# A mixture-of-experts layer whose tokens are selected by products on TensorE instead of gathered

## The reference

```
h2 = RMSNorm(x) * (1 + scale2) + shift2
lg = h2 @ w_rg                       # 4 groups: top 1
le = h2 @ w_re[group]                # 8 experts in the group: top 2
gates = softmax(lg)[group] * softmax(top 2 of le)
for each expert e with its tokens:
    hdn = silu(xe @ w_gate[e]) * (xe @ w_up[e])     # 1024 -> 512
    y   = hdn @ w_down[e]                            # 512 -> 1024
x += gate2 * sum of gates * y over each token's two experts
```

## Time and profile before

| | |
|---|---|
| time, median of 2 runs | 1788.38 us (1786.84 to 1789.93) |
| the profiled execution | 1790.88 us, span 1789.1 us, mean granted clock 0.967 |
| TensorE products, weight loads | 1587.5 us (89%), 769.3 us (43%) |
| VectorE, ScalarE, GpSimd | 716.6 us (40%), 434.7 us (24%), 160.1 us (9%) |
| HBM read, written | 520.96 MB, 23.86 MB: 305 GB/s over the span |

### The profile page before, as it was taken

One profiled execution on the slowest core, in us unless ns is written; L12 is line 12 of the kernel. 1 busy time (PEld: TensorE's weight loads), 2 busy tenths in 40 slices (PEclk: granted clock), 3 DMA queues, 4 the chain that ended last, 5 costly groups with the idle time before them and its releaser, 6 DMA issues.

```text
span 1789.1 us, 22316 instructions
## 1 busy us (share of the span) xinstructions
PE 1587.5 (89%) x7460; PEld 769.3 (43%) x7460; DVE 716.6 (40%) x1461; ACT 434.7 (24%) x995; POOL 160.1 (9%) x184
## 2 busy tenths in 40 slices
PE   5999999998998998888889999999899989887883
PEld 2455645463333343333345555455433333333331
DVE  1577466672222212122157855743522222222124
ACT  2111467112111111111121016741111112111112
POOL 0000000111111011111000000001110111111010
PEclk9999999989999999999989999999999999999997
DMA  9625532479999999999972365213899999999995
GB/s 360 236 71 189 211 116 95 162 285 367 407 397 403 408 406 399 412 410 414 368 280 94 116 214 197 82 48 109 316 402 399 402 412 403 407 412 401 398 410 199
DMA packets 124293, 528.44 MB, mean 295 GB/s; under 512 B 17184, under 2 KB 23328, under 8 KB 77568
## 3 DMA queue, kind: packets, MB, share of 16 engines
q1 hardware_dynamic: 106704, 491.46, 70.1%
q0 software_dynamic: 12480, 24.51, 4.3%
q10 hardware_dynamic: 4976, 10.55, 1.6%
HBM read 520.96 MB, written 23.86 MB: 305 GB/s over the span
## 4 chain that ended last, share of the span: by engine, by line
PE 65%; DMA 13%; SPq 9%; DVE 5%; ACT 4%; issue 4%; ACTq 0%; DVEq 0%; POOLq 0%
PE ps L1411 24%; PE ps L1050 18%; DMA ring<-in_w_exp_up 7%; PE ps L1263 6%; SPq L870 6%; PE ps L1409 4%; PE ps L1205 2%; SPq L860 2%; PE ps L1219 2%; PE ps L1245 2%; DMA arena<-in_w_exp_up 2%; ACT arena L1688 2%; ACT arena L1702 1%; DMA hT<-in_w_exp_up 1%; DMA ring<-in_w_in 1%
## 5 line engine op out<-in xcount | busy, mean ns | idle before, releaser
L1411 PE MATMUL ps<-ring,arena 128*64 128x512 f32 x1728 | 490.7, 609 | 48.6 <-ACT arena L1702 29.9
L1411 PEld LDWEIGHTS ps<-ring,arena 128*64 128x64 f32 x1728 | 158.2, 140 | 280.8 <-issue 270.6
L1050 PE MATMUL ps<-ring,hT 128*128 128x512 f32 (+1 forms) x768 | 254.8, 487 | 2.9 <-DMA ring<-in_w_in 1.9
L743 DVE TENSOR_TENSOR arena<-ps,arena 64x512 f32<-64x512 f32 (+1 forms) x64 | 44.4, 693 | 458.5 <-ACT arena L1696 380.1
L1696 ACT ACTIVATE arena<-ps 128x512 f32<-128x512 f32 x64 | 38.2, 597 | 756.3 <-PE ps L1411 705.5
L1050 PEld LDWEIGHTS ps<-ring,hT 128*128 128x128 f32 x768 | 144.3, 190 | 102.7 <-issue 91.0
L751 DVE TENSOR_TENSOR arena<-ps,gate 64x512 f32<-64x512 f32 (+1 forms) x64 | 43.7, 683 | 283.2 <-PE ps L1411 263.1
L1015 POOL DMA_INDIRECT yexp_d<-arena,masks x64 | 59.7, 932 | 838.3 <-DVE arena L753 775.0
L1411 PE MATMUL ps<-home,arena 128*64 128x512 f32 x320 | 122.3, 601 | 11.1 <-ACT arena L1702 5.1
L1411 PE MATMUL ps<-work,arena 128*64 128x512 f32 x288 | 111.2, 613 | 9.1 <-ACT arena L1702 5.1
L1411 PE MATMUL ps<-hT,arena 128*64 128x512 f32 x272 | 107.5, 613 | 7.8 <-ACT arena L1702 4.7
(11 more groups left out here) (233 smaller groups left out, 1734.7 us busy)
## 6 DMA issues: line engine op xcount, KB each, us to landing
ring<-in_w_exp_up SPq DMA_DIRECT2D x80, 1024.0 KB
ring<-in_w_exp_down SPq DMA_DIRECT2D x78, 1024.0 KB
ring<-in_w_exp_gate SPq DMA_DIRECT2D x74, 1024.0 KB
ring<-in_w_ada SPq DMA_DIRECT2D x24, 2048.0 KB, 11.0
ring<-in_w_in SPq DMA_DIRECT2D x8, 2048.0 KB, 21.9
home<-in_w_exp_gate SPq DMA_DIRECT2D x16, 1024.0 KB
hT<-in_w_exp_down SPq DMA_DIRECT2D x12, 1024.0 KB
work<-in_w_exp_gate SPq DMA_DIRECT2D x12, 1024.0 KB
```

Source lines behind the costliest of these rows:

```text
L1050: last = pe.matmul(out, lhs(k), rhs(k), start=(k == 0), stop=(k == n - 1))
L1411: last = [pe.matmul(outs[c][HALF * c:HALF * c + HALF, :], lhs(k)[:, 0:HALF], rhs(c, k), start=(k == 0), stop=(k == n - 1), tile_position=( ...
```

## The change

No expert's rows are gathered. Instead VectorE makes, for each expert, four 128x128 blocks `picks` (one for each token tile): row i, column r holds the token's 1/rms if token i has slot r of this expert, otherwise zero. It compares `iota` with `places_of`, which is the token's rank for each expert it has, and −1 for the others, and multiplies with `rstd`. TensorE then multiplies `x` itself with them (`pick_tokens`): for each of the eight column blocks k four products over the token tiles, added up in PSUM. The result lies where the transposes put theirs, in banks 3 and 4, and everything after it is as before. The two buffers `picks` lie where `xg` was.

Around it: the first pick stands right behind the ranks on TensorE, ahead of the lists and `mods(1)`; `more_lists` moves behind expert 1's pick; idle products ahead of the first two experts go (two of 512 columns remain in layer 1). On VectorE the first expert's drain moves into `route`, the gate factors move into `rest`, behind expert 1's tokens; `gidx` is made only for the second lists. GpSimd only scatters. SP loads the first unit of `work` after the lists, behind the first two loads of the second round.

```diff
+        picks = [arena[:, S * j:S * j + S].rearrange("p (t r) -> p t r", t=TT) for j in range(2)]
+        places_of = z[:, 1, 360:360 + TT * NE].rearrange("p (t e) -> p t e", t=TT)
...
+        def pick(dve, e, j):
+
+            for t in range(TT):
+                at = places_of[:, t, e:e + 1] if isinstance(e, int) else places_of[:, t, bass.ds(e, 1)]
+                last = dve.tensor_scalar(picks[j][:, t, :], C["iota"], at, rstd[:, t:t + 1], ALU.is_equal, ALU.mult)
+            last.then_inc(pick_ready, 1)
...
+            link(dve.scalar_tensor_tensor(places_of, rk, 1.0, hots, ALU.add, ALU.mult))
+            link(dve.tensor_scalar(places_of, places_of, -1.0, None, ALU.add))
+            dve.wait_ge(xn_out, 16 * TT * (l + 1))
+            pick(dve, 0, 0)
...
             with dve.Fori(1, HE - 1) as it:
+                expert_pick(2 * it + 2, 0)
                 expert_rows(2 * it, it, 0)
                 expert_hidden(2 * it + 1, it, 1)
                 expert_tokens(2 * it + 2, 0)
+                expert_pick(2 * it + 3, 1)
...
-                        sp.wait_ge(xg_in[0], 16 * (l * HE + 1))
+                        await_filled(sp, (l, "lists"))
...
-                for m in range(NBUF):
+                def first_load(m):
...
-                for m in range(NBUF, 3 * TURN):
+                for m in range(NBUF - 1):
+                    first_load(m)
+                for m in range(NBUF, NBUF + 2):
+                    expert_unit(0, m)
+                first_load(NBUF - 1)
+                for m in range(NBUF + 2, 3 * TURN):
                     expert_unit(0, m)
...
-                for e in range(2):
-                    gather(e)
                 for e in range(NE):
-                    if e + 2 < NE:
-                        gather(e + 2)
                     scatter(e)
...
-                def turn_tokens(q, n):
+                def pick_tokens(q, n):
                     e, j = expert(q, n), n % 2
-                    pe.wait_ge(xg_in[j], 8 * TURN * q + 16 * (l * HE + n // 2 + 1))
+                    pe.wait_ge(pick_ready, NE * l + e + 1)
                     for half in range(2):
                         b = 3 + half
                         await_bank_free(b, e)
-                        for q in range(4):
-                            k = 4 * half + q
-                            last = pe.transpose(bank_e(b).rearrange("p (a s) -> p a s", a=4)[:, q, :], xg[j][:, k:D:KD], ident)
+                        for i in range(4):
+                            k = 4 * half + i
+                            for t in range(TT):
+                                last = pe.matmul(bank_e(b)[:, P * i:P * i + P], x[:, t, k:D:KD], picks[j][:, t, :],
+                                                 start=(t == 0), stop=(t == TT - 1))
                         last.then_inc(filled[b], 1)
```

More of the change, by code:

```diff
@@ L326, in program @@
         v = {g: arena[:, 6144 + 1024 * i:7168 + 1024 * i].rearrange("p (t c) -> p t c", t=TT) for i, g in enumerate(GROUPS)}
-        xg = [arena[:, D * j:D * j + D] for j in range(2)]
+        xg = arena[:, 0:D]
         xgT = arena[:, 2048:2048 + D].rearrange("p (k s) -> p k s", k=KD)
@@ L693, in route @@
             slot_of_rank().then_inc(slots_ready, 1)
[L695 to L711, removed]
             def rest():
@@ L763, in experts_dve @@
             expert_tokens(2, 0)
+            expert_pick(3, 1)
             expert_rows(1, 0, 1)
@@ L993, in _, with scatter @@
                 pool.wait_ge(xn_out, 16 * TT * (l + 1))
-                for j in range(2):
-                    link(pool.memset(xg[j], 0.0))
                 words = wide_words(pool, l)
-                def gather(e):
+                def scatter(e):
                     def body(w):
                         if e == 0:
[L1002 to L1012, removed]
+                            pool.wait_ge(rows_ready, l + 1)
                         pool.wait_ge(drained[5], expert_bank(l, 5) + e + 1)
@@ L1457, in down @@
                     by_width(pe, words, TURN // 2 * q + n // 2, j, body)
+                pick_tokens(0, 0)
+                key = (l, "list_parts")
+                pe.wait_ge(slots_ready, 2 * l + 1)
+                await_free(pe, key)
+                for r in range(2):
+                    for q in range(4):
+                        last = pe.matmul(bank(key)[NE * q:NE * q + NE, 0:P], slot_val[:, 4 * r + q, 0:NE], slot_hot[:, 4 * r + q, :],
+                                         start=(r == 0), stop=(r == 1), tile_position=(0, NE * q))
+                fills(last, key)
+                if ADA_NEXT[l]:
+                    mods(1)
+                else:
+                    idle_products(2, 1)
+                key = (l, "lists")
+                await_free(pe, key)
+                fills(pe.matmul(bank(key)[:, 0:NE], list_parts, C["fold32"], start=True, stop=True), key)
                 words = wide_words(pe, l)
-                turn_tokens(0, 0)
-                idle_products(1, 1)
                 gate_up(0, 0)
-                turn_tokens(0, 1)
+                pick_tokens(0, 1)
+                key = (l, "more_lists")
+                pe.wait_ge(slots_ready, 2 * l + 2)
+                await_free(pe, key)
+                fills(product(bank(key)[:, NE:P], lambda n: slot_hot[:, n, :], lambda n: slot_val[:, n, NE:P], n=2 * TT), key)
                 with pe.Fori(0, NE // TURN) as q:
```

55 lines of the change are left out of this document (37 added, 18 removed).

## The result

The changed kernel takes 2591.3 us (median of 2 runs, 2589.2 to 2593.4), against 1788.4: a ratio of 1.449 (95% interval 1.447 to 1.452). I had forecast slower, 2084, within 2056 to 2150. The sign was right, the size was not: +803 us where I had +296.

A forecast was written before the change was run, and what follows sets the result against it. Weights' DMA and TensorE were taken to bind closely, TensorE alone after the change. Layer middles +139.8 and +127.3, last picks +11.4, starts +10.4 and +6.6 sum to +295.5 us: 2084 us, range 2056 to 2150.

The forecast's parts named there:

- What bounds the kernel: Expert phases: weights' DMA and TensorE lie close together; TensorE waits for weights only 66 us in the whole kernel.
- The records: Pick products on TensorE: each expert's 32 products are recorded twice, 64 records, 4096 in all.
- The price of a record: Pick products on TensorE: 0.110 us each, upper end 0.126, making a pick 7.3 us.
- the turns of the loop: TensorE's loop over ten experts turning back: the prediction had no term for it.
- the forecast's own case: Whole kernel: picks of 64 records at 0.110 us make TensorE bind; 2084 us, chance 0.87.
- The two middles: Each layer from expert 2's pick to expert 31's: 581.1 us (+139.8) in layer 0, 570.7 (+127.3) in layer 1.
- The 0.28 us that I put behind each pick: End of each pick on TensorE: 0.28 us until the next product can start, added to 64 records.
- The first pick of layer 0: Start of layer 0's expert phase: 10 us for TensorE's partly halved clock, gate and up starting at 409.4.
- Gathers at nothing: POOL's gathers go with their DMA traffic; as TensorE binds, that gives nothing.
- third rival: Expert picks: no slower if a pick hides in the weights' wait, at most 2.5 us; 1760 us, chance 0.03.
- (1): Pick products: weight load and stream run one after the other, 0.217 us a record; 2522 us, chance 0.05.
- (2): Pick products: recorded once each, a pick 3.8 us; +72 us, about 1860, chance 0.05.

The follow-up runs named there:

- e16: The kernel before the change with TensorE's loop over ten experts written out three times: 1788.0 us, ratio 1.000.
- e1_blocks: The changed kernel with 128 neighbouring features as x's stationary block in place of every eighth: 2107.8 us.
- e7_32_transposes: The changed kernel with each pick's 32 products replaced by 32 transposes of the same blocks of x, nothing selected: 1890.5 us.
- e17_blocks_unrolled: e1_blocks with TensorE's loop over ten experts written out three times: 2072.0 us.
- e4: The changed kernel with only 64 of the selection's 128 columns streamed in each pick product: 2770.0 us.
- e9_bf16: The changed kernel with the selection in bfloat16 and only the upper 16 bits of x read, still 32 bytes apart: 1781.3 us, ratio 0.996.
- e14: e9_bf16 with TensorE's loop over ten experts written out three times: 1744.9 us, ratio 0.976.
- e12_every_3rd: The changed kernel with every third feature (12 bytes apart) in x's stationary block in place of every eighth: 2340.2 us.
- e3_every_4th: The changed kernel with every fourth feature (16 bytes apart) in x's stationary block in place of every eighth: 2561.9 us.
- e11_two_gathers: The kernel before the change without the gathers of experts 2 to 31 in each layer, nor waits for them: 1738.5 us, ratio 0.972.
- e2: The changed kernel with every second feature (8 bytes apart) in x's stationary block in place of every eighth: 2119.4 us.

## Why the prediction was wrong

**What bounds the kernel:** right in kind. With weights and TensorE a few per cent apart any work on TensorE would show. But of the 66 us that I called a wait for weights, some 21 were the turns of the loop; e16 shows that this made no difference to that kernel, since the weights take what the turns leave.

**The records:** right, 32 products are 64 records, 4096 in all.

**The price of a record: the step that failed.** "I take 0.110, the row of 96 columns". All rows from which I bounded it have contiguous blocks; the new product's block has its elements 32 bytes apart. With contiguous blocks the pace is (7.41 − 0.28)/63 = 0.113 in e1_blocks, so the argument from 36, 96 and 256 columns was sound for what it compared. The only rows at 32 bytes were the transposes, and I read them as the price of the shape with an upper end of 0.126; e7_32_transposes shows that they cost 0.122 at a distance at which a product's record costs 0.242. The measured 0.240 gives 64 x 64 x (0.240 − 0.110) = +532 us on my sum, 2616, against 2591 measured. The profile's clue was there, in the operands of the diff (`x[:, t, k:D:KD]`), not in a row.

**A term at nothing without a reason: the turns of the loop.** In the changed kernel they cost 0.2 us each, so nothing was lost by it; in the forecast's own case, e1_blocks, they cost 31 us.

**Everything else in the sum** is 12 us too high: e17_blocks_unrolled, which has nearly my price (0.113) and no turns, takes 2072 against 2084. The two middles take 575.0 and 564.5 us there where I had 581.1 and 570.7. The 0.28 us that I put behind each pick was not there: in e1_blocks the next product starts 7.25 us after the pick's start, 64 x 0.113. The narrow expert was 19.2 us where I had 19.3; in the changed kernel the waits for weights vanished; the wait of 0.84 us for ScalarE stayed; VectorE's selection was never waited for in the loop. The first pick of layer 0 I had lengthened to 10 us for the half clock; it took 15.55, as all do, and gate and up began at 413.5 where I had 409.4.

**Gathers at nothing:** this fits the changed kernel, where TensorE never waits for the experts' loads; no run puts the gathers back into it. As the prize of the third rival I had 30 us, for 12 MB at 405 GB/s. The gathers were only 8.4 MB (24.51 in the queue before, 16.11 after), and yet they are worth 50 us.

**Rivals.** (1), load and stream one after the other, gave 2522 and lies nearest to the time, and is wrong all the same, so that this nearness is luck: e1 keeps both operands' sizes and costs half, e4 halves the stream and costs the same. The rule of the Trainium skill ("TensorE: Matmul & The Clock Gate", Part 3, The mechanism) that LDWEIGHTS overlaps with products only across row groups is not borne out by e1: 0.1165 us a record, while the prices that the rival gives to a load and a stream, 0.109 and 0.108, would add up to 0.217. (2) fell with the count of records. (3) had its threshold right: with picks of 2.2 us, under the 2.5 I had worked out, e9_bf16 is no slower than the kernel before, and with picks of 3.7 e7_32_transposes is, at 1890.

## What to carry to other kernels

Before a row gives the price of a product, compare the addresses, not just the shape: the stationary operand of a float32 product wants its elements at most 8 bytes apart, since 16 and 32 bytes double the record (0.1165 us to 0.237 and 0.242), and a streamed operand at 32 bytes costs the same (0.237). Test an edit without its costly part: here that showed 50 us of gain under 852 of loss, and a cheaper product (one record instead of two, at lower precision) made the idea a gain of 2.4%. Where two limits lie close together, what a saving on one of them is worth depends on the other: the loop's turns were worth nothing beside the gathers (e16), and 36 us without them (e9 to e14).

## What the runs showed of the hardware

- The pace of the float32 products whose block has its elements 32 bytes apart does not follow TensorE's clock: 0.24 us a record at a granted clock of 0.60 and 0.23 at 1.00. That of the bfloat16 records of e9_bf16 does: 0.107 us from start to start at 0.50, 0.064 at 1.00.
- Streaming 64 in place of 128 columns in records bound by the read let the granted clock fall from 1.00 to 0.70 over the phase and cost 179 us (e4_64_moving, one run).
- Upper halves of float32 numbers, 32 bytes apart, read as bfloat16: 0.0705 us a record; the same blocks as float32: 0.242 each for two records.
- A turn of TensorE's long loop made its interval longer by 7.5 to 8.9 us in e9_bf16, by 3.0 to 5.3 in e12_every_3rd, and by 0.2 in e3_every_4th and in the changed kernel (27.45 us against 27.27). How busy the DMA is does not order these: e11_two_gathers, with its DMA full, loses 3.9 to 4.8, e1_blocks, with a DMA share of 0.85, 6.7 to 8.3. Among the loops with 64 records a pick, the loss shrinks as the pick that ends the loop's body grows: pick and loss together are 14 to 17 us in e1 (7.3 us of pick), e2 (7.6), e12 (11.3) and e3 (15.0). That TensorE fetches the loop's first instructions while it works on the pick would fit; no run here shows it.
- The kernel with gathers moved 406 GB/s in all in the stretch shown, without them 419; 8 MB of gathers cost 50 us of time.
